# Seven block products in every down unit of a ConvFFN, each down unit set between two up units

## The reference, cut to what matters

```
def conv_ffn(h, w_up, conv_w, conv_b, w_down, buf):
    z = h @ w_up
    T = z.shape[1]
    zp = jnp.concatenate([buf.astype(z.dtype), z], axis=1)
    zc = conv_b + sum(zp[:, j:j + T] * conv_w[j] for j in range(CONV_W))
    g, a = jnp.split(zc, 2, axis=-1)
    y = (jax.nn.silu(g) * a) @ w_down
    return y, zp[:, -(CONV_W - 1):]
...
    x = x + mix.astype(dt)
    f, new_buf = conv_ffn(rmsnorm(x, norm2), w_up, ffn_conv_w, ffn_conv_b, w_down, conv_buf)
    x = x + f.astype(dt)
```

## Time and profile before

| what | before |
|---|---|
| time, median of 3 runs | 2228.49 us (2226.58 to 2231.26) |
| time of the profiled execution | 2225.15 us |
| its span | 2223.4 us |
| PE busy | 2196.5 us, 99% of the span |
| DVE, POOL, ACT busy | 1105.3 (50%), 1027.2 (46%), 787.9 (35%) us |
| mean granted clock of TensorE | 0.998 |
| chain that ended last | PE 92%, issue 3%, POOL 2% |

### The profile page before, as it was taken

How to read it: one execution, slowest core, us unless ns; L and a number is a source line. 1 busy time by engine, 2 the same in 40 slices (tenths; PEclk the granted TensorE clock), 3 DMA queues, 4 the chain that set the end, 5 groups by cost and what they waited for, 6 DMA issues and landing times.

```text
span 2223.4 us, 45330 instructions
## 1 busy us (share of the span) xinstructions
PE 2196.5 (99%) x18098; PEld 2135.1 (96%) x18098; DVE 1105.3 (50%) x1755; ACT 787.9 (35%) x1337; POOL 1027.2 (46%) x788
## 2 busy tenths in 40 slices
PE   8999999989999999999999999999999999999999
PEld 7999888988899999999999999999999999999999
DVE  5122457266643565563645636456464554635364
ACT  5223343245544333333333333333333333333231
POOL 5443333332244445455454645545455464554452
PEclk9999999999999999999999999999999999999999
DMA  7532223642222433323233332333323233233323
GB/s 224 129 94 76 60 68 85 110 144 77 63 82 71 116 95 96 96 75 109 81 98 92 94 96 78 111 94 97 96 83 99 85 97 93 94 94 97 95 86 114
DMA packets 325080, 213.65 MB, mean 96 GB/s; under 512 B 12744, under 2 KB 299441, under 8 KB 324081
## 3 DMA queue, kind: packets, MB, share of 16 engines
q1 hardware_dynamic: 322121, 211.27, 33.8%
q10 hardware_dynamic: 2880, 1.26, 0.3%
HBM read 201.37 MB, written 11.49 MB: 96 GB/s over the span
## 4 chain that ended last, share of the span: by engine, by line
PE 92%; issue 3%; POOL 2%; ACT 1%; DVE 1%; DMA 1%; POOLq 0%; SPq 0%; ACTq 0%
PE ps L510 56%; PE ps L886 10%; PE ps L881 9%; PE ps L758 8%; PE ps L857 2%; POOL wlo L1995 1%; PE ps L797 1%; PE ps L817 1%; PE ps L807 1%; DMA xtok<-in_x_prompt 0%; PE ps L627 0%; ACT act_hi L1028 0%; PE ps L636 0%; PE ps L635 0%; DMA raw<-in_w_in 0%
## 5 line engine op out<-in xcount | busy, mean ns | idle before, releaser
L997 ACT ACTIVATE whi<-raw 128x512 fp32r<-128x512 f32 x632 | 393.4, 630 | 961.8 <-PE ps L510 756.4
L2032 POOL TENSOR_TENSOR wlo<-raw,whi 128x512 fp32r<-128x512 f32 x336 | 452.2, 1350 | 477.1 <-ACT whi L997 475.9
L1995 POOL TENSOR_TENSOR wlo<-raw,whi 128x512 fp32r<-128x512 f32 x200 | 260.0, 1302 | 450.8 <-ACT whi L997 450.8
L510 PE MATMUL ps<-h_hi,whi 128*128 128x260 f32 x2816 | 395.7, 283 | 0.0
L510 PE MATMUL ps<-h_lo,whi 128*128 128x260 f32 x2816 | 394.0, 282 | 0.0
L510 PE MATMUL ps<-h_hi,wlo 128*128 128x260 f32 x2816 | 393.2, 282 | 0.0
L510 PEld LDWEIGHTS ps<-h_hi,whi 128*128 128x128 f32 x2816 | 361.2, 188 | 0.4
L510 PEld LDWEIGHTS ps<-h_lo,whi 128*128 128x128 f32 x2816 | 360.9, 188 | 0.0
L510 PEld LDWEIGHTS ps<-h_hi,wlo 128*128 128x128 f32 x2816 | 360.6, 188 | 0.0
L2044 POOL TENSOR_TENSOR wlo<-raw,whi 128x512 fp32r<-128x512 f32 x140 | 193.4, 1385 | 123.0 <-ACT whi L1322 64.2
L1853 DVE TENSOR_TENSOR za<-ps,rs 128x520 f32<-128x520 f32 x44 | 30.8, 700 | 363.9 <-PE ps L510 363.9
(11 more groups left out here) (358 smaller groups left out, 3141.4 us busy)
## 6 DMA issues: line engine op xcount, KB each, us to landing
raw<-in_w_up SPq DMA_DIRECT2D x88, 1024.0 KB, 5.7
raw<-in_w_down SPq DMA_DIRECT2D x44, 1024.0 KB, 5.0
raw<-in_w_in SPq DMA_DIRECT2D x30, 1024.0 KB, 5.7
raw<-in_w_out SPq DMA_DIRECT2D x64, 256.0 KB, 3.9
x_spill<-xT SPq DMA_DIRECT2D x1, 4160.0 KB, 16.4
xtok<-in_x_prompt SPq DMA_DIRECT2D x4, 1024.0 KB, 8.4
out_y_prompt<-ytok SPq DMA_DIRECT2D x3, 1024.0 KB
xT<-x_spill SPq DMA_DIRECT2D x1, 2860.0 KB, 10.8
```

Source lines behind the costliest of these rows:

```text
L510: mm = nc.tensor.matmul(ps[:, bank + h, 0:NH], w[:, k, c, :], x[:, 4 * c + k, h * NH:(h + 1) * NH], start=(k == 0 and kind == 0 and c == 0 ...
L997: nc.scalar.activation(whi[:, k, :, :], rawq(k, slot), ACT.Copy)\
L1995: nc.gpsimd.tensor_tensor(wlo[:, k, :, :], rawq(k, u), whi[:, k, :, :].bitcast(F32), ALU.subtract).then_inc(w_lo, 1)
L2032: nc.gpsimd.tensor_tensor(wlo[:, k, :, :], rawq(k, u % 2), whi[:, k, :, :].bitcast(F32), ALU.subtract).then_inc(w_lo, 1)
```

## The change

All four down units are units of seven, and a down unit stands between two up units. `SEQ` gives the order in the loop: u0 u1 d0 u2 d1 u3 d2 u4 d3 u5 u6 u7. In the last group `SEQ_LAST` is u0 u1 d0 u2 d1 u3 d2 u4 u5 u6 u7 d3, then e0 to e3. The bank pairs of the pieces go by unit: B first and D second for even m, D first and B second for odd m, so that the second piece takes the bank pair of the up unit just ahead. The weight sums (four tiles now instead of three, with s4 of its own) are made in one go by DVE during the up unit in front. Two products that are added at two places each (p2, p3) are now one DVE instruction each, with the product broadcast. The gated values' own blocks of which no product is made are no longer split. The diff, cut:

```
-SEVEN = (False, True, False, True)
...
+SEQ = ("u0", "u1", "d0", "u2", "d1", "u3", "d2", "u4", "d3", "u5", "u6", "u7")
+SEQ_LAST = ("u0", "u1", "d0", "u2", "d1", "u3", "d2", "u4", "u5", "u6", "u7", "d3", "e0", "e1", "e2", "e3")
...
-    PRODUCTS = [(BANK_B, 0), (BANK_D, 5), (BANK_A, 4), (BANK_C, 6), (BANK_B, 2), (BANK_A, 3), (BANK_C, 7)]
-    WEIGHTS = [("a", 0, 0), ("s", 1), ("s", 0), ("s", 2), ("a", 0, 1), ("s", 1), ("a", 1, 1)]
+    BLOCKS = [0, 4, 3, 5, 1, 2, 6]
+    BANKS = [[BANK_B, BANK_D, BANK_A, BANK_C, BANK_B, BANK_A, BANK_C], [BANK_D, BANK_B, BANK_A, BANK_C, BANK_D, BANK_A, BANK_C]]
+    WEIGHTS = [("a", 0, 0), ("s", 1), ("s", 0), ("s", 2), ("a", 0, 1), ("s", 3), ("a", 1, 1)]
...
+        def down_unit(m, q, l, low, ev0, use0, last=False):
+
+            for p in range(PIECES):
+                k, bank, last_q = p % 4, down_bank(m, p, last), last_use(m, p, last)
+                pe.wait_ge(w_hi, q + (p + 1))
+                if last_q is not None:
+                    pe.wait_ge(s("d_ev"), ev0 + (last_q + 1))
+                if p == 0 and m == 0:
+                    pe.wait_ge(z_free, use0 + 3)
+                if p == 0 and last and m == 3:
+                    pe.wait_ge(z_free, use0 + 9)
+                if p == 1:
+                    pe.wait_ge(z_free, use0 + (10 if last and m == 3 else m + 4))
...
+        def group_units(seq, q0, l0, low, ev0, use0, q_at, l_at, last=False):
...
+                if 2 <= u <= 5 and not (last and u == 5):
+                    pe.wait_ge(s("d_ev"), ev0 + (PIECES * (u - 2) + 5))
+                pe.wait_ge(z_free, use0 + (u + 1))
+                up_mm(l0 + l_at[name], 2 * (u % 2))
...
+        def take_product(q, ev, m, p, last):
...
+            elif p == 2:
+                ins = tt(tiles[:, :, :, 1, :], both, tiles[:, :, :, 1, :], add)
             elif p == 3:
-                tt(down_tiles(m, 1, 0), src, down_tiles(m, 1, 0), add)
-                ins = tt(down_tiles(m, 1, 1), src, down_tiles(m, 1, 1), add)
+                ins = tt(tiles[:, :, 1, :, :], both, tiles[:, :, 1, :, :], add)
...
+        def weight_sums(made, m, slot, landed):
...
+            dve.wait_ge(raw_in[slot], landed)
+            for i, (to, x, y, op) in enumerate(((s1, a21, a22, add), (s2, s1, a11, sub), (s3, a11, a21, sub), (s4, a12, s2, sub))):
...
+            mixed_lo(1, True)
+            read_unit(0)
+            sums_of(0)
+            conv(n0, 0, 0)
+            read_unit(1)
+            products(0)
+            sums_of(1)
+            conv(n0, 1, 0)
+            gate(n0, 0)
+            read_unit(2)
+            products(1)
...
+            if ends:
...
+                products(3, {0: lambda: conv(n0 + 3, 1, 3), 1: lambda: gate(n0 + 3, 3), 3: lambda: last_lo(0),
+                             4: lambda: last_lo(1), 5: lambda: last_lo(2), 6: lambda: last_lo(3)})
...
+                sp.wait_ge(w_lo, split + 4 + l_at[older] + (LOWS if older[0] == "d" else 4))
```

More of the change, by code:

```diff
@@ L878, in down_unit @@
                     for i in range(2):
[L879 to L888, removed]
+                        for g in range(2):
+                            mm = nc.tensor.matmul(ps[:, bank + g, 0:NH], w[:, k, 2 * i + g, :], x[:, i, BLOCKS[p], :],
+                                                  start=(kind == 0 and i == 0), stop=(kind == 2 and i == 1))
@@ L1340, in ffn_group_act @@
             n0 = grp * GC
[L1341 to L1364, removed]
@@ L1365, in ffn_group_act @@
                     if j == 2:
-                        due.setdefault((g + 3, 3), []).append((mixed_hi, grp * 2, 0))
+                        due.setdefault((g + 3, 3), []).append((mixed_hi, 0, 0))
             at_piece = 4
             back = 0
-            for u in range(1, units + (0 if ends else 1)):
-                m = u - downs[0] if downs[0] <= u < downs[1] else None
-                seven = m is not None and SEVEN[m]
+            for u in range(1, len(seq)):
+                m = int(seq[u][1]) if seq[u][0] == "d" else None
@@ L1379, in ffn_group_act @@
                     at_piece += 1
-                    if ends and (u, k) == (U_GRP + 3, 0):
+                    if ends and (u, k) == (12, 1):
                         read_tail()
[L1382 to L1385, removed]
-                back = 1 if seven else 0
+                    for step, x, j in due.get((u, k), []):
+                        step(grp * 2 + x if step is mixed_hi else n0 + x, j)
@@ L1388, in _ @@
+                back = 0 if m is None else 1
         n_group = 0
@@ new lines, in read_unit, with gate_of, split_of @@
+            def read_unit(u):
+                off = q_at[f"u{u}"] if with_down or ends else 4 * u
+                read(n0 + u // 2, u % 2, off, u // 2)
+            def gate_of(j):
+                conv(n0 + j, 0, j)
+                conv(n0 + j, 1, j)
+                gate(n0 + j, j)
+            def split_of(j):
+                lo(n0 + j, j)
+                if j >= 2:
+                    mix(j - 2)
+                if j == 2:
+                    mixed_lo(0, False)
+            if not (with_down or ends):
+                for j in range(GC):
+                    read_unit(2 * j)
+                    read_unit(2 * j + 1)
+                    gate_of(j)
+                    split_of(j)
+                return told[0]
@@ new lines, in ffn_group_dve @@
+            mixed_lo(1, True)
[9 more added lines that the diff above has]
+            products(1)
+            sums_of(2)
+            conv(n0 + 1, 0, 1)
+            read_unit(3)
+            products(2)
+            if not ends:
+                sums_of(3)
+            conv(n0 + 1, 1, 1)
+            gate(n0 + 1, 1)
```

330 lines of the change are left out of this document (156 added, 174 removed).

## The result

The changed kernel takes 2256.65 us in the median (2252.83 to 2259.22), against 2228.43 us for the kernel before in the same session (2226.58 to 2231.26): a ratio of 1.0124 (95% interval 1.0105 to 1.0143), or 28.2 us more. The forecast was slower by 11.6 us with a range up to 2256: the sign was right, the loss more than twice as large, and the time just past the upper end.

What follows compares the result with a forecast made beforehand. PE was taken as dense to the matmul and so the bound. From the profiled 2225.15 us, - 29.4 + 39 + 2.0 gave 2236.8, or 2240 us for the median; own range 2233 to 2247, wider range 2224 to 2256.

Steps and rivals of the forecast that it cites:

- Matmuls removed: d0 and d2 become units of seven in ten groups: 20 units, each 1.47 us shorter, 29.4 us gained.
- rival 1: The stall at p1 does not come, so the change is faster: 2201 us; chance 0.13.
- The wait that is moved: p1 of a down unit waits on `z_free` behind u1 to u4: 1.0 us, 39 times, 39 us lost.
- The last group's end: d3 directly follows u7, so DVE has more work before PE's last units: 2.0 us lost, between 0 and 5.
- Edits costed at nothing: Weight sums, extra splits, DVE's merged products and SP's queue of loads: each taken as covered, cost 0.
- rivals 3 and 4: Rival 3: second wait in down units, 2250 to 2256, chance 0.14; rival 4: DVE late at u2 and u4, 2268, 0.04.
- rival 3: POOL holds `weight_low`, p6 waits for p3's product in down units: 10 to 16 us more, 2250 to 2256; chance 0.14.
- the other reading of the merged products: Merged DVE products take turns with POOL: PE loses some 0.4 us in each of 40 units, 16 us, 2256.

Runs made afterwards that it cites:

- e0: Not a run: the first of the units e0 to e3 that follow d3 at the end of the last group; no time of its own as a run.
- both cures: Changed kernel with p1 waiting for DVE's read, not the small copy, and PE's down/up rounds rolled into a loop again; 2200.65 us, 0.9870 of the kernel before.
- e3_rolled: Changed kernel with d0 u2 d1 u3 and d2 u4 d3 u5 as two rounds of an inner PE loop, p1's wait kept; 2237.52 us, 1.0034.
- e6_unrolled: Changed kernel with PE's loop over the FFN groups written out, so nothing jumps back, p1's wait kept; 2240.18 us, 1.0042.
- after kept busy: Changed kernel with 24 unread matmuls added ahead of the last group's tail transposes; one profiled execution, 2251.07 us.

## Why the prediction came out as it did

- **Matmuls removed, -29.4 us: right.** The profile has 240 fewer (18098 to 17858), 12 in each of 20 units, at the pace that was read. With both cures the kernel stands at 2200.65 us, and rival 1, the removed matmuls without the stall, was worked out as 2201. That the two meet so closely is in part luck: rival 1 has 2.0 us for the last group's end in it, and with both cures PE waits 1.5 us less there than in after.
- **The wait that is moved, +39 us: right in mechanism and nearly in size.** Copy and split end within 0.02 us of each other, PE waits at p1 behind u1 to u4 in each group. In the loop a unit is 0.94 us longer, not 1.0, and in the last group 1.07: 36 x 0.94 + 3 x 1.07 = 37.0. Taking the wait away gave 41.4 us between medians, and 37.1 between spans (2251.0 and 2213.9), with 1.0 of the gain in the clock of the last group.
- **The last group's end, +2.0 us: right in kind, 0.6 too much.** From d3's first matmul (2172.60) to e0 (2188.53) it took 15.9 us, where I had 16.5, so the term measured 1.4. Of the 4.2 us that the last group grew, 2.5 are the clock; the rest is this term and three waits of 1.07, less two units of 1.47.
- **Edits costed at nothing: right for those named.** No wait of the loop goes to the weight sums, to the merged products or to the next up unit's splits, so rivals 3 and 4 did not come. What rival 3 feared for `weight_low` did come in most units, without a wait of PE: it took 1.39 us in the median, where before the median was 0.68.

```profile
L1823 DVE TENSOR_TENSOR wlo<-sums,whi x40: 681/1389/1394, 833.5 to 2180.4; 128x512 fp32r<-128x512 f32 x40
```

  The merged products, which no row of before showed, took what was assumed, 1.24 us, and the 40 of each kind differ by less than 0.01 us beside POOL's work (ns min/median/max):

```profile
L1802 DVE TENSOR_TENSOR xT<-ps,xT x40: 1241/1242/1243, 832.3 to 2179.2; 128x1040 f32<-128x1040 f32 x40
```

```profile
L1804 DVE TENSOR_TENSOR xT<-ps,xT x40: 1226/1228/1234, 834.8 to 2181.0; 128x1040 f32<-128x1040 f32 x40
```

  The Trainium skill's rule that was weighed there (SBUF — State Buffer, "Who interferes with whom": one SBUF input, no contention with GpSimd) is borne out by these rows.
- **What failed: the list of edits was not complete.** The step "Edits that I cost at nothing, and their cover" follows what the change does on ACT, POOL, DVE and SP, and leaves out that the diff turns PE's inner loop into straight code. I took the writing-out as the way in which the order is told, not as an edit. Put at nothing, it costs eight pauses, 12.4 us, and eight units slower by some 0.25, 2.0: 14.4 us; by itself, in the kernel before, it cost 15.5 between medians. The measured time lies next to the 2256 that rival 3 and the other reading of the merged products came to; that is chance, since neither of their waits is in the trace. No row of before shows such a pause, but its page has the 58 packets of the instruction queue, and the kernel after could be counted before it ran.

The account closes in the spans: forecast +11.6; pauses +14.4; shorter waits at p1, 37.0 - 39 = -2.0; shorter end of the last group -0.6; clock of the last group in these two profiles +2.5; the front of the program +1.5, which no part of the change touches and which moves as much in other profiles (816.80 instead of 813.24 for the kernel before profiled again). The sum is 27.4 against 27.6 measured. Without the pauses the median would have come out near 2240: `e3_rolled` and `e6_unrolled`, two ways to be rid of them with the wait left in, measure 2237.52 and 2240.18, where 2240 was forecast.

## What to carry to other kernels

Where a diff writes a loop out or adds units to a loop's body, count the instructions of that body on each engine, weight loads among them, and watch the instruction queue: a body that is no longer held costs a pause at every jump back, and then rolling part of it up, or having no jump, is worth more than most edits of the work inside. Before a wait is moved close to its release, look at what raises the semaphore: here a copy of ten columns that nobody on the path needed stood between a finished read and PE, and POOL set its length; let the consumer wait for the read itself. A gain in matmuls counts only once the waits and pauses that come with it are paid for: the same 29.4 us made the kernel 1.2% slower, and 1.3% faster with the two losses taken away.

## What the runs showed of the hardware that I had not expected

- A jump back to instructions of PE that are no longer held stopped it for 1.4 to 1.9 us, until 1.6 to 1.8 us behind the end of an instruction packet, and the next unit of 96 matmuls took 11.73 us, not 11.49. Straight code whose instructions stream in all the while (131 packets) had no pause.
- The same 128x10 values took 1.05 us in the median as a copy from SBUF beside POOL's splits, each ending with the POOL instruction that it met, and 0.17 us as a product from PSUM beside the same splits.
- TensorE's granted clock fell to 0.50 behind 3.2 us without matmuls in one execution of the kernel before and stayed at 1.00 in another; it cost up to 2.6 us. In the second profile of after, and in that of after kept busy, it fell to 0.50 behind one of the loop's pauses (1.80 and 1.96 us), and the unit behind took 13.28 us instead of 11.73.
